# Two transformer blocks in one kernel: a new order for the second block's attention

## What is computed

```python
h = rmsnorm(x, ln_mix_g) * (1 + sc1) + sh1             # x: output of the first block, with its final norm
q, kc, vc, ksl, vsl, kw, vw, gts, cb, cc, ch = split(h @ w_in)
kc, vc = compress(kc), compress(vc)                    # windows of 32 tokens, stride 16, gelu between two matrices
o_cmp = softmax(q kc + bias) vc                        # 15 compressed keys
o_slc = softmax(q ks + bias) vs                        # selected blocks: with 256 tokens all 4 are selected
o_win = softmax(q kw + bias) vw                        # window of 512: all earlier tokens
o_attn = g0 * o_cmp + g1 * o_slc + g2 * o_win          # g = sigmoid(gts)
o_conv = cb * conv3(cc * ch)
x = x + gt1 * (concat(rmsnorm(o_attn), rmsnorm(o_conv)) @ w_out)
x = x + gt2 * peer_ffn(rmsnorm(x, ln_ffn_g) * (1 + sc2) + sh2)
```

## Time and profile before

| | |
|---|---|
| median of 3 runs | 1243.81 us (1243.55 to 1246.93) |
| span of the profiled execution | 1243.2 us |
| the second block's first projection starts | 282.39 us |
| the sums of the first norm behind its attention start | 394.65 us |
| busy over the span: TensorE, VectorE, ScalarE, GpSimd | 96%, 72%, 62%, 46% |

### The profile page before, as it was taken

The page is one execution under the profiler, slowest core; times in us unless marked ns, Lnnn a source line. Parts: engine busy times, 40 slices in busy tenths (PEclk is TensorE's granted clock), DMA queues, the critical chain, the costliest instruction groups (busy, mean ns, idle before and its releaser), DMA issues.

```text
span 1243.2 us, 27547 instructions
## 1 busy us (share of the span) xinstructions
PE 1198.1 (96%) x8800; PEld 1103.0 (89%) x8800; DVE 889.3 (72%) x1833; ACT 768.2 (62%) x1730; POOL 567.3 (46%) x505
## 2 busy tenths in 40 slices
PE   8999999988897999999999999999999999999997
PEld 8989988988887999999999999999888888888885
DVE  5776768889575839992688888860576767686766
ACT  5446676465665555557777788875555555555554
POOL 3664543435464348988877777778200000000000
PEclk9999999999999999999999999999999999999999
DMA  6668656538633445555576666668676576767663
GB/s 236 226 204 301 226 200 198 168 117 311 237 120 119 136 135 172 184 179 177 189 216 207 203 200 214 200 209 272 196 245 210 190 256 188 256 195 257 189 198 103
DMA packets 85826, 249.84 MB, mean 201 GB/s; under 512 B 8019, under 2 KB 29692, under 8 KB 84988
## 3 DMA queue, kind: packets, MB, share of 16 engines
q1 hardware_dynamic: 77356, 209.62, 53.2%
q0 software_dynamic: 8400, 39.34, 8.5%
HBM read 237.38 MB, written 13.12 MB: 202 GB/s over the span
## 4 chain that ended last, share of the span: by engine, by line
PE 84%; DVE 7%; ACT 4%; issue 3%; DMA 2%; POOL 1%; DVEq 0%; ACTq 0%; SPq 0%; POOLq 0%
PE psum L684 83%; DMA ring<-v_rows 2%; ACT w_hi L1171 1%; DVE s_sb L1751 1%; DVE w_lo L1737 1%; DVE arena L1790 1%; PE psum L883 0%; DVE rstd L1731 0%; ACT arena L1328 0%; ACT arena L1154 0%; DVE arena L1946 0%; DVE xres L1871 0%; POOL arena L1650 0%; DVE arena L1852 0%; ACT L1328 0%
## 5 line engine op out<-in xcount | busy, mean ns | idle before, releaser
L1567 POOL TENSOR_TENSOR w_lo<-ring,w_hi 128x512 fp32r<-128x512 f32 x368 | 492.1, 1348 | 277.2 <-ACT w_hi L1171 266.5
L1171 ACT ACTIVATE w_hi<-ring 128x512 fp32r<-128x512 f32 x734 | 445.2, 627 | 274.7 <-PE psum L684 263.8
L684 PE MATMUL psum<-h_hi,w_hi 128*128 128x256 f32 x1832 | 534.5, 292 | 21.8 <-DVE w_lo L1737 7.4
L684 PE MATMUL psum<-h_lo,w_hi 128*128 128x256 f32 x1832 | 520.8, 284 | 0.0
L684 PE MATMUL psum<-h_hi,w_lo 128*128 128x256 f32 x1832 | 520.3, 284 | 0.0
L684 PEld LDWEIGHTS psum<-h_hi,w_hi 128*128 128x128 f32 x1832 | 353.2, 193 | 36.1 <-issue 23.1
L684 PEld LDWEIGHTS psum<-h_lo,w_hi 128*128 128x128 f32 x1832 | 353.6, 193 | 0.3
L684 PEld LDWEIGHTS psum<-h_hi,w_lo 128*128 128x128 f32 x1832 | 353.3, 193 | 0.0
L1737 DVE TENSOR_TENSOR w_lo<-ring,w_hi 128x512 fp32r<-128x512 f32 x238 | 188.6, 793 | 130.7 <-ACT w_hi L1171 130.1
L684 PE MATMUL psum<-w_hi,h_hi 128*128 128x512 f32 (+1 forms) x592 | 224.2, 379 | 4.4 <-ACT w_hi L1171 1.8
L684 PE MATMUL psum<-w_hi,h_lo 128*128 128x512 f32 (+1 forms) x592 | 222.2, 375 | 0.0
(11 more groups left out here) (214 smaller groups left out, 1126.5 us busy)
## 6 DMA issues: line engine op xcount, KB each, us to landing
ring<-u_t SPq DMA_DIRECT2D x128, 512.0 KB, 3.6
ring<-v_rows SPq DMA_DIRECT2D x128, 512.0 KB, 3.6
ring<-weights SPq DMA_DIRECT2D x115, 512.0 KB, 4.1
arena<-mods POOLq DMA_DIRECT2D x48, 512.0 KB, 5.5
routing_weights<-s_sb SPq DMA_DIRECT2D x32, 320.0 KB, 4.2
s_sb<-routing_weights POOLq DMA_DIRECT2D x5, 2048.0 KB, 10.3
bias_rows<-bias_row POOLq DMA_DIRECT2D x1, 1536.0 KB, 11.4
xres<-x_t SPq DMA_DIRECT2D x2, 512.0 KB, 4.6
```

What stands on the lines that cost most here:

```text
L684: return nc.tensor.matmul(out, lhs, rhs, start=start, stop=stop, **kw)
L1171: nc.scalar.activation(w_hi[:, half, :], src, ACT.Copy).then_inc(hi_done, 1)
L1567: nc.gpsimd.tensor_tensor(w_lo[:, half, :], src, w_hi[:, half, :].bitcast(F32), ALU.subtract)\
```

## The change

The step list of the second block is written anew. Of the ten projections nq0, nq1, gt and ks run ahead of the first scores; kw, kc, vc, nq2, nq3 and nv come between the steps of pairs 8 to 10 and of compression. A list `side` holds vectors 26 to 33, x1 1 to 8 and vectors 34 to 39, in this order; one comes behind each of these projections, then one or two in each pair, up to pair 15. The fillers all lie behind cmps: one in pairs 14 and 15, two in pairs 9 to 13. The waits of scores and cmps for q and k, the place of the sigmoid's table load (now behind gt), the buffers of vectors 34 to 39 (MERGED is read longer now) and the places of their loads and of the bias sheet's load (now at `ple`, before the first block's merge) follow from it.

```diff
+    steps += [("norm", 2), ("proj", "nq0"), ("proj", "nq1"), ("x1", 0)]
+    for step in ("gt", "ks", ("gates",), ("scores", 8), "kw", ("soft", 8), ("scores", 9), "kc", ("soft", 9), "vc",
+                 ("turn", 8), ("scores", 10), "nq2", ("cmpk",), ("cmpv",), ("soft", 10), "nq3", ("cmpk1",), ("cmpv1",),
+                 "nv", ("cmps",)):
+        steps += [step] if isinstance(step, tuple) else [("proj", step), side.pop(0)]
+        steps += [side.pop(0)] if step == "nv" else []
...
             if m >= MODS_C:
                 return flat(120, 4), 4
+            if m >= MODS_B:
+                return flat((SIG + 8, SIG + 12, PLE + 2, PLE + 6)[(m - MODS_B) % 4], 4), (m - MODS_B) % 4
...
-            if s in (("soft", 8), ("soft", 9)):
-                return SPLIT[SLOT_AT[("proj", "cc0")]]
             if s[0] == "soft":
                 later = [x for x in STEPS[STEPS.index(s):] if x[0] == "proj"]
+                if s[1] in (8, 9, 10):
+                    return SPLIT[SLOT_AT[later[0]]]
                 return ahead(later[0]) if later else -1
-            if s == ("scores", 9):
-                return SPLIT[SLOT_AT[("proj", "cc0")]]
-            if s == ("proj", "gt"):
-                return SPLIT[SLOT_AT[("proj", "cc0")]]
...
-                        pe_.wait_ge(a_read, filled("proj", "kw"))
+                        pe_.wait_ge(a_read, max(filled("proj", f"nq{(p - 8) // 2}"), filled("proj", ("ks", "kw")[p % 2])))
...
                 elif s == ("gates",):
-                    pool.wait_ge(x1_ready, KC)
...
-                elif s == ("proj", "vc"):
-                    pool.wait_ge(sheet_in, 32)
-                    pool.wait_ge(turn_done, 8)
-                    skew = bass.AP(bias_dram.tensor, bias_dram.offset + P - 1,
-                                   [[HEADS * TRI - 1, P], [TRI, HEADS], [1, T]])
-                    pool.dma_start(sheet, skew).then_inc(sheet_in, 16)
-                elif s == ("cmpk",):
+                elif s == ("x1", 1):
                     for m in range(MODS_B, MODS_B + 3):
                         load_mod(m)
...
                     for m in range(MODS_A, MODS_O):
                         load_mod(m)
+                    pool.wait_ge(sheet_in, 32)
+                    pool.wait_ge(turn_done, 8)
+                    skew = bass.AP(bias_dram.tensor, bias_dram.offset + P - 1,
+                                   [[HEADS * TRI - 1, P], [TRI, HEADS], [1, T]])
+                    pool.dma_start(sheet, skew).then_inc(sheet_in, 16)
```

More of the change, by code:

```diff
@@ L69 @@
     + [f"{n}{b}" for n in ("mq", "mk") for b in range(4)] + ["mv"]
-FIRST2 = [f"nq{b}" for b in range(4)] + ["kc", "vc", "ks", "kw", "nv", "gt"]
 SLOTS_OF = {"dv": 4, "mv": 4, "nv": 2}
@@ L98, in plan @@
     assert not mod
-    mod = list(range(MODS_O, MODS_C))
+    side = [("mod", m) for m in range(MODS_O, MODS_B)] + [("x1", c) for c in range(1, 9)] \
+        + [("mod", m) for m in range(MODS_B, MODS_C)]
     steps += [("ple",), ("merge",), ("out1",), ("gate",)]
[L101 to L105, removed]
+    steps += [("norm", 2), ("proj", "nq0"), ("proj", "nq1"), ("x1", 0)]
[4 more added lines that the diff above has]
+        steps += [side.pop(0)] if step == "nv" else []
     fill = [("proj", n) for n in FILL2]
-    steps += [("scores", 8), ("gates",), ("scores", 9), ("soft", 8), fill.pop(0), ("soft", 9), ("cmpk",), ("cmpv",),
-              ("turn", 8), ("scores", 10), fill.pop(0), ("cmpk1",), ("cmpv1",), ("soft", 10), fill.pop(0), ("cmps",)]
     for p in range(9, 16):
-        steps += {10: [("z", 0), ("z", 1)], 12: [("z", 2)], 14: [("z", 3)]}.get(p, [])
+        steps += {10: [("z", 0)], 11: [("z", 1)], 13: [("z", 2)], 14: [("z", 3)]}.get(p, [])
         steps.append(("turn", p))
@@ L113, in plan @@
             steps.append(("scores", p + 2))
-        if p < 15:
-            steps.append(("mod", mod.pop(0)))
+        steps.append(side.pop(0))
         if p + 2 < 16:
             steps.append(("soft", p + 2))
-        steps += {10: [("conv", 0)], 11: [("cgate", 0), ("conv", 1)], 12: [("csq", 0)], 13: [("conv", 2), ("cgate", 1)],
-                  14: [("conv", 3), ("csq", 1)], 15: [("cgate", 2), ("csq", 2)]}.get(p, [])
+        steps += {10: [("conv", 0)], 11: [("conv", 1)], 12: [("cgate", 0)], 13: [("conv", 2), ("csq", 0), ("cgate", 1)],
+                  14: [("conv", 3), ("csq", 1)], 15: [("cgate", 2)]}.get(p, [])
+        if p == 14:
+            steps.append(side.pop(0))
         steps.append(fill.pop(0))
@@ L122, in plan @@
             steps.append(("cmpt",))
-        if p in (9, 12):
-            steps.append(fill.pop(0))
+        if p < 14:
+            steps += [side.pop(0), fill.pop(0)]
         if p in (9, 11, 13):
             steps.append(("pv", p))
+    assert not side
+    steps.append(("csq", 2))
     steps += [("cgate", 3), ("csq", 3), ("pv", 15), ("mix", 0)]
@@ L973, in _ @@
                 elif kind == "cmps":
-                    pe_.wait_ge(a_read, filled("cmpk", 1))
+                    pe_.wait_ge(a_read, max(filled("cmpk", 1), filled("proj", "nq3")))
                     pe_.wait_ge(pt_done, 9)
```

5 lines of the change are left out of this document (3 added, 2 removed).

## The result

| | before | after |
|---|---|---|
| median | 1244.13 us (1243.55 to 1246.93, 4 runs) | 1252.25 us (1251.01 to 1253.66, 4 runs) |
| span of the profiled execution | 1243.2 | 1249.9 |

The ratio is 1.006 with a 95% interval of 1.0046 to 1.0074. Forecast were 1244.0 us, with "same" (1240.1 to 1247.5) as the likeliest; 1252.25 lies above the range of 1238.5 to 1249.0 as well. The result is slower.

The account below looks back on a forecast made before the run. TensorE, busy 96% of the span, was taken to bound the kernel. Terms +3.3 +0.6 -1.4 -2.75 +0.5 gave +0.25 on 1243.2, so 1243.5 profiled and 1244.0 us as median; range 1238.5 to 1249.0.

Parts of the forecast that it names:

- Up to the end of cmps: First part of the stretch, from 293.24: waits of 6.8 us against 3.4 before, kept as +3.3, plus +0.6 for low clock.
- NQ3: Projection behind cmpk/cmpv: waits 1.85 us for cmpk's bank, which the gelu frees and nothing covers now.
- cmpv1: Matmuls behind NQ3: wait 1.9 us for NQ3's bank, whose evacuation on ScalarE stands behind soft 10 and its exp table.
- VC: Projection behind KC: waits 1.5 us for VectorE's low half, made after soft 8 and the maxima of scores 9.
- NV: Double projection before cmps: second bank waits 0.45 us for cmpv1's four-piece evacuation; some of it may run at low clock, +0.6.
- From cmps to the second filler: Second part: turn 9 waits 0.95 instead of 1.79, CH0's low half is the late one; 8.0 against 9.35 us, -1.4.
- The pairs: Third part: waits of 0.9 for three low halves, 1.35 in pair 13, 0.6 at CB3; 2.85 against 5.6 us, -2.75.
- pair 13: In the pairs: a vector (1.45 us) between maxima and low half makes TensorE wait 1.35, as at 371.08 before.
- CB3: End of the pairs: the wait of 3.42 us shrinks to 0.6 (0 to 1.5), given 3 us more cover behind scores 15.
- The sheet: The 1,024 KB load behind ple's vector loads delays merge's weights: +0.5 us, bounds 0 and 4.5; slower rival's chance 0.09.
- backlog rival: In the pairs x1 steps on top of VectorE's work lose 8.8 us instead of 2.85: 1250.0 in all; chance 0.17.
- The table's drain: Rival: two more pauses of 1.38 us for table changes between cmpk and NV: 1246.8; chance 0.02.

Follow-up runs that it names:

- a_ahead: Changed kernel without the special case of soft 8 to 10, so weight halves are made before the exps and probabilities there; 1253.03 us, ratio 1.0071.
- a_tail: Changed kernel with z 3, conv 3 and csq 1 moved behind CB2, nothing else; 1248.68 us, ratio 1.0033.
- a_mended: Changed kernel with the sheet's load at norm 2, halves ahead of soft 8 to 10 early, z 3, conv 3, csq 1 behind CB2; 1245.52 us, 1.0011.
- a_side_late: Changed kernel with the side step of pairs 9 to 13 put behind soft instead of ahead of it; 1250.84 us, ratio 1.0052.
- b_spread: Kernel before with its own order, only the side work spread as in the change and the sheet's load at norm 2; 1244.36 us, ratio 1.0000.
- a_x1_early: Changed kernel with x1 1 to 8 and vectors 26 to 33 back behind projections KS to NV, vectors 34 to 39 in pairs 9 to 14; 1250.55 us, 1.0046.
- a_m_fill: a_mended with the side step of pairs 9 to 13 behind soft, plus unread matmuls ahead of NQ3, cmpv1, turn 9 and CB3; 1243.36 us, ratio 0.9994.
- b_tail: Kernel before with z 3, conv 3 and csq 1 moved behind CB2; 1240.02 us, ratio 0.9963.
- b_spread_tail: Kernel before with the side work spread, and z 3, conv 3 and csq 1 behind CB2; 1242.22 us, ratio 0.9978.
- a_sheet_norm: Changed kernel with the bias sheet's load moved to norm 2; 1250.47 us, ratio 1.0048.
- b_tail_fill: b_tail with 8 matmuls that nobody reads added ahead of turn 9; 1240.89 us, ratio 0.9974.

## Why the prediction was wrong

It failed by size and in one place by mechanism. By its own parts:

- **Up to the end of cmps**: +3.3 and +0.6 were forecast, +5.7 measured. The steps were right as a list, and the waits that come from evacuations and the table hit well: scores 8 0.26 (0.14), scores 9 0.47 (0.45), cmpk 0.56 (0.5), NQ3 1.81 (1.85), cmpv1 1.84 (1.9). Missed was one for halves, VC: 2.35 instead of 1.5. The prediction followed the lower half on VectorE only. The upper half on GpSimd, behind soft 8, was late as well, and the special case in `ahead` that puts it there stands in the diff. a_ahead showed it: 1.6 less in this part. NV lost 1.4, with the low clock where it was forecast, against 0.45 for the bank and 0.6 for the clock; behind it a wait for halves was hidden, which shows in a_tail (0.33 and 0.75), whose NQ3 and not NV has the low clock, and is gone in a_mended (6.53 for NV). 0.4 are in the short matmuls.
- **From cmps to the second filler**: -1.4 forecast, -0.6 measured. The 0.95 at turn 9 was right. The low clock held on through most of CC0 (7.48 us from 338.55 to 346.03 for 4.6 us of work), so TensorE and not CH0's low half set the end: 8.77 instead of 8.0.
- **The pairs**: this is the step that failed. -2.75 was forecast and +1.2 measured, 4.0 of the 6.6 us by which the stretch was missed. 0.3 for each of three pairs was 0.47, pair 13's 1.35 was 2.71 and another 1.49 for the low clock in CH3, CB3's 0.6 was 1.53. The 1.35 was carried over from a place where the vector ran in 1.45; here it took 3.72. The vectors that the x1 steps displace were not priced either: five of them now lie behind scores 15, where there were two. And "CC3, CH3 and pv 13 lie behind scores 15, 3 us more cover" took the chain as fixed and the cover as new. The chain grew with it: the probabilities of soft 15, behind that vector and the low half, start at 385.45, 6.8 behind scores 15 (378.62), where before it was 5.4 (374.76 to 380.17). Worse, the parts are not independent: what a_side_late wins between scores 15 and CB3 is lost at CB3, and what a_ahead and b_spread win ahead of scores 15 is lost through a longer chain and the low clock behind it, so that the sum of parts on which the forecast rests did not hold.
- **The sheet**: 0.5 forecast, 1.1 to 1.4 measured, within its bounds, and the mechanism was as told.
- **The range**: it ended at 1249.0, though the text's own bound for the sheet gives 1248.0, and it left out the backlog rival's 1250.0 with its chance of 0.17. 1252.25 lies above all of them.
- **The table's drain**: not there. The gelu, the exp and the sigmoid tables load in 1.28 with nothing idle behind; the waits between cmpk and NV came out at what 1.3 gives.

The rival "VectorE's backlog in the pairs" (1250.0) had the right sign and the right engine, but not the whole: a_x1_early takes the x1 steps out of the pairs, has four waits of 1.3 for low halves there in their place, and is only 1.7 faster, a difference within the two intervals. The four kernels before, b_spread, a_x1_early and after show that most of the loss comes with early attention, as long as nothing else is mended.

How much of it is early attention itself is open. With the chain mended in both kernels (1.0033 and 0.9963) they are 8.7 us apart. Sheet and halves are 2.7 of it, the side steps behind scores 1.5, the low clock 0.6 to 1.9, by differences that are partly within the intervals. Left are 2.6 (by the stretch) to 3.9 (by the ratios) between a_m_fill and b_tail. By the pieces this rest does not lie ahead of scores 15. a_m_fill is there after 92.84, with the one projection that it has less there 95.89, and b_tail after 96.02: its waits at scores 8 and 9, turn 8, the gelu's bank and cmpv1 (0.25, 0.47, 0.98, 1.9 and 2.1 with the filling) are no more than what b_tail loses in other places. The rest lies at CH3 (0.98) and CB3 (2.33 with the filling). Ahead of CH3 the low half itself takes 2.72 beside GpSimd, ahead of CB3 it stands behind vectors of 2.50 and 2.15; b_tail has no wait there. b_spread_tail, with the old order and side work spread, shows the same in part: 2.8 sooner at scores 15 than b_tail, 3.3 lost behind it. So the side work at the end of the pairs is what these traces point to for the rest, and no run here moved it away in the changed order with everything else mended.

## What to carry to other kernels

When a reordering is judged, follow both halves of every operand through both engines that make them, and ask of each wait which chain it ends, and where that chain starts: one that starts at scores 15 and ends at CB3 takes back what is won between the two, and a long wait at its end costs the clock as well. An edit that "does nothing" may only be hidden by such a chain: look for the wait that has grown in its trace, take that away first, and try the edit again. To see it, cut the trace at a few landmarks and compare the pieces, not only the total. And before an order is rewritten, look for the longest wait in the old one: moving three steps past one projection won 4.5 us, which the rewriting of ten projections did not.

## What the runs showed of the hardware

- Instructions of VectorE and GpSimd that ran side by side took longer, by far more than one instruction's length in some places. A vector that takes 1.27 alone took 3.72 next to GpSimd instructions in a row, and ended 1.10 after the last of them; x1 took 0.47 and 1.50, the latter ending 0.29 after GpSimd's low half (355.43). It can also be GpSimd that gets longer: its low half took 1.28 and 2.24, its four scalings 1.62 to 3.54, and next to one of these a vector took only 1.38. A duration taken from another neighbourhood is no price.
- Behind idle times of 0.95, 1.84 and 2.71 us matmuls ran 0.21 apart for 3 to 6.4 us, at a granted clock of 0.50 to 0.62, thus mostly at 1.2 GHz. Behind the wait of 1.81 ahead of NQ3 the same order of work gave the low clock in one trace (a_tail: NQ3 4.54) and the full one in another (after: 3.07), with the low clock at NV instead. Behind the same 0.95 turn 9 ran at the low clock in after and a_ahead and at the full one in a_tail, a_mended and a_sheet_norm. So a wait alone does not tell whether the clock falls. Matmuls whose result nobody reads kept it at 1.00. In b_tail_fill that won nothing, since another engine was late just behind; in a_m_fill 0.6 to 1.9.
- A change of ScalarE's function table took 1.28, and the next instruction started 0.01 to 0.02 behind it; between the matmuls of cmpk and those of cmpv1 two such changes are on TensorE's path.
